# The scan of a hybrid backbone: where the next tile's raw products, its loads and the turned output stand

## The reference, cut to what matters

```python
def step(S, inp):
    r_t, w_t, k_t, v_t, kk_t, kka_t = inp
    sa = jnp.einsum('bdhvk,bdhk->bdhv', S, kk_t)
    S = (S * w_t[..., None, :] - sa[..., :, None] * kka_t[..., None, :]
         + v_t[..., :, None] * k_t[..., None, :])
    return S, jnp.einsum('bdhvk,bdhk->bdhv', S, r_t)
...
y = ys[:, :, 0] + jnp.flip(ys[:, :, 1], axis=1)
mu = jnp.mean(y, axis=-1, keepdims=True)
var = jnp.mean(jnp.square(y - mu), axis=-1, keepdims=True)
yn = ((y - mu) * lax.rsqrt(var + GN_EPS)).reshape(B, T, C) * lnx_w + lnx_b
```

## Time and profile before

| | us |
|---|---|
| median of 3 runs (4039.37 to 4051.58) | 4044.41 |
| the profiled execution, whole | 4038.96 |
| its span, first to last instruction | 4037.1 |
| scan stage, about | 955 to 1983 |
| merge stage, about | 1983 to 3240 |

### The profile page before, as it was taken

One profiled execution on the slowest core, in us unless ns is written; L12 is line 12 of the kernel. 1 busy time (PEld: TensorE's weight loads), 2 busy tenths in 40 slices (PEclk: granted clock), 3 DMA queues, 4 the chain that ended last, 5 costly groups with the idle time before them and its releaser, 6 DMA issues. The chain is left out here.

```text
span 4037.1 us, 64429 instructions
## 1 busy us (share of the span) xinstructions
PE 3634.8 (90%) x24967; PEld 2874.3 (71%) x24968; DVE 1380.7 (34%) x2811; ACT 748.8 (19%) x1399; POOL 1173.0 (29%) x1677
## 2 busy tenths in 40 slices
PE   8999999995688889889799999999999959999960
PEld 4666666663688888888788898998998944444430
DVE  2444444443344444444212222222122241222227
ACT  1222222222222322232101111111111001111113
POOL 0333333334566556655211101101101000000013
PEclk9999999997899999999899999999999969999985
DMA  8333323323332333232441101111111135665226
GB/s 286 105 104 104 104 99 104 104 85 107 95 94 60 97 100 92 62 97 74 144 171 40 63 35 40 63 35 45 58 40 54 50 119 197 241 232 192 94 101 216
DMA packets 297255, 424.33 MB, mean 105 GB/s; under 512 B 122446, under 2 KB 206156, under 8 KB 297036
## 3 DMA queue, kind: packets, MB, share of 16 engines
q1 hardware_dynamic: 278028, 351.79, 26.3%
q0 software_dynamic: 11952, 43.52, 3.3%
q10 hardware_dynamic: 7056, 25.69, 1.6%
HBM read 287.99 MB, written 132.94 MB: 104 GB/s over the span
## 5 line engine op out<-in xcount | busy, mean ns | idle before, releaser
L1761 PE MATMUL c_ps<-c_hT,big 128*128 128x128 f32 x6528 | 752.5, 276 | 25.3 <-DMA big<-in_w_in 25.3
L1761 PEld LDWEIGHTS c_ps<-c_hT,big 128*128 128x128 f32 x6528 | 743.8, 193 | 33.2 <-issue 29.5
L661 PE MATMUL a_ps<-a_win,a_hT 128*128 128x512 f32 (+1 forms) x1088 | 416.1, 540 | 3.5 <-DVE a_mix L572 3.5
L2184 PE MATMUL e_ps<-big,e_xT 128*128 x784 | 347.6, 597 | 2.3 <-DVE e_xT L2146 2.3
L661 PEld LDWEIGHTS a_ps<-a_win,a_hT 128*128 128x128 f32 x1088 | 204.1, 190 | 199.4 <-issue 187.0
L655 PE MATMUL a_ps<-a_hT,a_win 128*128 128x128 f32 x2992 | 343.5, 277 | 2.3 <-ACT a_hT L343 2.3
L655 PEld LDWEIGHTS a_ps<-a_hT,a_win 128*128 128x128 f32 x2992 | 340.2, 193 | 6.1 <-issue 2.9
L1095 POOL TENSOR_TENSOR b_tmp<-b_tt,b_ta 128x126 f32<-128x126 f32 (+22 forms) x527 | 203.1, 385 | 321.4 <-DMA b_ta<-s_a 266.7
L2184 PEld LDWEIGHTS e_ps<-big,e_xT 128*128 128x128 f32 x784 | 149.4, 191 | 191.7 <-issue 191.7
L1761 PE MATMUL c_ps<-c_wo,c_mT 128*128 128x512 f32 x544 | 236.3, 592 | 0.0
L1726 DVE TENSOR_TENSOR c_gs<-c_gs,c_ps 128x384 f32<-128x384 f32 x136 | 75.4, 554 | 444.8 <-PE c_ps L1761 434.5
(11 more groups left out here) (327 smaller groups left out, 5379.6 us busy)
## 6 DMA issues: line engine op xcount, KB each, us to landing
big<-in_exp_w SPq DMA_DIRECT2D x48, 1024.0 KB, 10.3
s_D<-a_shared SPq DMA_DIRECT2D x34, 768.0 KB, 5.8
b_f<-s_D SPq DMA_DIRECT2D x34, 768.0 KB, 7.2
s_yr<-e_yo ACTq DMA_DIRECT2D x49, 512.0 KB, 3.2
b_f<-s_A SPq DMA_DIRECT2D x34, 512.0 KB, 5.7
a_aw<-in_ada_w SPq DMA_DIRECT2D x32, 512.0 KB, 6.7
s_A<-a_shared SPq DMA_DIRECT2D x17, 768.0 KB, 3.4
big<-in_w_in SPq DMA_DIRECT2D x12, 1024.0 KB, 12.5
```

The source lines that it names most:

```text
L661: ins = nc.tensor.matmul(ps[:, bank, 0:width], hT[b][:, k, :], win[:, k, c:c + width], start=k == 0, stop=k == KD - 1)
L1761: return nc.tensor.matmul(out, lhsT, rhs, start=start, stop=stop)
L2184: return nc.tensor.matmul(out, lhsT, rhs, start=start, stop=stop)
```

## The change

It has four parts.

1. **The next tile's raw product stands at the head of a tile.** PE turns b and q of tile q+1, then r and k of tile q, forms `raw(q + 1)`, and then arb, aqk and ark of tile q. `b_ar` and `b_bT` have a second buffer each (`each2`); r goes through bank 0, k through bank 2, xx through bank 1. DVE transposes `b_ar` (AT) between the arb masks and the aqk masks. SP sends the diagonal blocks out right behind the inverse.
2. **`load_front` stands on ACT's queue**, in `front`, after `identity` and ahead of `b_xs`; it waits there for the same three things as on SP.
3. **The masked blocks**: AL5 is a plain copy of four 32-row blocks on ACT (`blocks`, after `b_u`), u6 reads `b_ar` itself, AL6 and POOL's `blocks` are gone.
4. **The output is made turned**: the moving operand of y is now the mix (`b_arkT`, `b_arbT`, 128 columns) and the weights are 64 columns of v or us; the two heads of a pair write to the two halves of PSUM's partitions. The stored tile is the transpose of before. In the merge, `turn_y` turns the sum of both directions back with four more transposes a tile; `scan_center` reads PSUM.

The diff, cut to its core:

```diff
-RT, BT, KT = each("rT", [P, 4, P]), each("bT", [P, 4, P]), each("kT", [P, 4, P])
-Ar, AT = each("ar", [P, H, P]), sb("b_at", [P, H, P])
-AL5, AL6 = each("al5", [P, H, P]), each("al6", [P, H, P])
+RT, KT, BT = each("rT", [P, 4, P]), each("kT", [P, 4, P]), each2("bT", [P, 4, P])
+Ar, AT = each2("ar", [P, H, P]), sb("b_at", [P, H, P])
+AL5 = each("al5", [P, H, P])
...
+def load_front(e, t, d):
+    e.dma_start(flat(F[d][:, 0:2, :]), tile_of(scr["A"], t)[:, 0:2 * W]).then_inc(f_in[d], 16)
+    e.dma_start(flat(F[d][:, 2:5, :]), tile_of(scr[f"D{d}"], t)).then_inc(f_in[d], 16)
...
             inverse_in(q)
+            if left > 0:
+                diagonal_out(q + 1, 1 - b)
...
-            if left > 1:
-                for d in range(2):
-                    sp.wait_ge(const_in, 48)
-                    after(sp, k_ok[d], q + 1)
-                    after(sp, b_ok[d], q + 1)
-                    after(sp, pm_ps[d], q + 1)
-                    load_front(two[d], d)
-            if left > 0:
-                diagonal_out(q + 1)
...
+        def front(t, tiles):
+            for d in range(2):
+                after(act, k_ok[d], t - 1)
+                after(act, b_ok[d], t - 1)
+                after(act, pm_ps[d], t - 1)
+                load_front(act, tiles[d], d)
...
+        def blocks(t, b):
+            for d in range(2):
+                for g in range(2):
+                    after(act, ar_ok[d][g], t)
+                    freed(act, u5_ps[d][g], t)
+                for c in range(2):
+                    first, second = slice(64 * c, 64 * c + 32), slice(64 * c + 32, 64 * c + 64)
+                    rows, cols = (second, first) if d == 0 else (first, second)
+                    a(AL5[d][rows, :, cols], Ar[d][b][rows, :, cols], ACT.Copy).then_inc(al5_ok[d], 1)
...
+            two = [tile_at(d, q + 2 if left > 2 else LAT) for d in range(2)]
+            if left > 2 and not isinstance(q, int):
+                two = [act.snap(t) for t in two]
             if left > 0:
                 turned(q + 1, 1 - b)
             for d in range(2):
+                after(act, kT_ps[d], q)
+                a(flat(KT[d][:, :, :]), bank(d, 2), ACT.Copy).then_inc(kT_ok[d], 1)
+            if left > 0:
+                raw(q + 1, 1 - b)
+                identity(q + 1)
+            if left > 1:
+                front(q + 2, two)
+            for d in range(2):
                 after(act, xx_ps[d], q)
-                a(Xs[d][:, :], bank(d, 0), ACT.Copy).then_inc(xs_ok[d], 1)
+                a(Xs[d][:, :], bank(d, 1), ACT.Copy).then_inc(xs_ok[d], 1)
+            for d, g in GROUPS:
+                after(act, u5_ps[d][g], q)
+                a(flat(U[d][:, heads(g), :]), bank(d, 2 * g), ACT.Copy).then_inc(u5_ok[d][g], 1)
             if left > 0:
-                raw(q + 1)
-                identity(q + 1)
+                blocks(q + 1, 1 - b)
...
+                if out is ArbT and left > 0:
+                    turn_raw(q + 1, 1 - b)
...
+            if isinstance(q, int) and q == 0:
+                for d, g in GROUPS:
+                    after(pe, ar_ok[d][g], 0)
+            if left > 0:
+                for d in range(2):
+                    turn_b(q + 1, 1 - b, d)
+                turn_q(q + 1, 0)
+            for d in range(2):
+                turn_r(d)
+            if left > 0:
+                turn_q(q + 1, 1)
+            for d in range(2):
+                turn_k(d)
+            if left > 0:
+                raw(q + 1, 1 - b)
+            for r in range(2):
+                for d in range(2):
+                    after(pe, (rT_ok, kT_ok)[r][d], q)
+                product(bT, RT, 2 * r, r, arb_ps)
+            for r in range(2):
+                for d in range(2):
+                    if left > 0:
+                        after(pe, ar_ok[d][in_round(d, r)], q + 1)
+                    else:
+                        freed(pe, (y_ok, pm_ok)[r][d], q + r)
+                product(KT, qT, 1 + 2 * r, r, aqk_ps)
...
-                    ins = mm(bank(d, 2)[lo, k * N:(k + 1) * N], AL6[d][hi, k, lo], TIT[d][hi, k, hi])
+                    ins = mm(bank(d, 2)[lo, k * N:(k + 1) * N], Ar[d][b][hi, k, lo], TIT[d][hi, k, hi])
...
-                    mm(bank(d, 1)[:, j * P:(j + 1) * P], RT[d][:, j, :], Shd[d][:, j, :], stop=False)
-                    for h in (2 * j, 2 * j + 1):
-                        own = slice(h * N, (h + 1) * N)
-                        mm(bank(d, 1)[:, own], ArkT[d][:, slot(h), :], V[d][b][:, own], start=False, stop=False)
-                        ins = mm(bank(d, 1)[:, own], ArbT[d][:, slot(h), :], Us[d][:, own], start=False, stop=h % 2 == 1)
+                    at = bank(d, 1)[:, j * P:(j + 1) * P]
+                    mm(at, Shd[d][:, j, :], RT[d][:, j, :], stop=False)
+                    for mix, val in ((ArkT, V[d][b]), (ArbT, Us[d])):
+                        for u in range(2):
+                            h = 2 * j + u
+                            ins = mm(at[64 * u:64 * u + 64], val[:, h * N:(h + 1) * N], mix[d][:, slot(h), :],
+                                     start=False, stop=mix is ArbT)
...
         def scan_center(t):
-            after(dve, s["ysum"], t)
-            v.reduce_sum(s8[0][:, :], by_head(ya[:, :]), axis=X_AXIS).then_inc(s["m_ok"], 1)
+            after(dve, s["yt_ps"], t)
...
+        def turn_y(t):
+            after(pe, s["ysum"], t)
+            freed(pe, s["yT_ok"], t)
+            for k in range(4):
+                ins = nc.tensor.transpose(ps[:, WB[1], k * P:(k + 1) * P], ya[:, k * P:(k + 1) * P], ident)
+            ins.then_inc(s["yt_ps"], 1)
...
+                if j == 2 and left > 0:
+                    turn_y(t + 1)
...
+                if i == 1 and left > 0:
+                    after(pe, s["yc_ok"], t + 1)
```

More of the change, by code:

```diff
@@ L880, in diagonal_out @@
                     after(sp, at_ok, t, 2)
-                    for d, tile in ((0, Ar[0]), (1, AT)):
+                    for d, tile in ((0, Ar[0][b]), (1, AT)):
                         for i in range(4):
@@ L929, in step @@
                     one = [tile_at(d, q + 1 if left > 1 else LAT) for d in range(2)]
-                    two = [tile_at(d, q + 2 if left > 2 else LAT) for d in range(2)]
                     past = [q - 1, 16 - q]
                     if left > 2 and not isinstance(q, int):
-                        one, two, past = ([sp.snap(t) for t in ts] for ts in (one, two, past))
+                        one, past = ([sp.snap(t) for t in ts] for ts in (one, past))
                     inverse_in(q)
+                    if left > 0:
+                        diagonal_out(q + 1, 1 - b)
                     for d in range(2):
@@ L993, in turned, with raw @@
                         a(flat(QT[d][b][:, :, :]), bank(d, 1), ACT.Copy).then_inc(qT_ok[d], 1)
-                    for d in range(2):
-                        after(act, bT_ps[d], t)
-                        a(flat(BT[d][:, :, :]), bank(d, 3), ACT.Copy).then_inc(bT_ok[d], 1)
-                def raw(t):
-                    freed(act, a_st, t, 128)
+                def raw(t, b):
+                    if not (isinstance(t, int) and t < 2):
+                        act.wait_ge(a_st, 128 * t - 128)
+                        for d in range(2):
+                            after(act, u6_ps[d], t - 2)
                     for r, pair in enumerate(PAIRS):
@@ L1019, in _ @@
                 turned(0, 0)
-                raw(0)
+                raw(0, 0)
+                act.wait_ge(clear_ok, 6)
+                blocks(0, 0)
+                front(1, [tile_at(d, 1) for d in range(2)])
                 for d in range(2):
@@ L1028, in step @@
                 def step(q, b, n, left):
-                    for d in range(2):
-                        after(act, kT_ps[d], q)
-                        a(flat(KT[d][:, :, :]), bank(d, 3), ACT.Copy).then_inc(kT_ok[d], 1)
+                    two = [tile_at(d, q + 2 if left > 2 else LAT) for d in range(2)]
+                    if left > 2 and not isinstance(q, int):
+                        two = [act.snap(t) for t in two]
                     if left > 0:
@@ L1042, in step @@
                             own_decay(q + 2, d)
-                    for d, g in GROUPS:
-                        after(act, u5_ps[d][g], q)
-                        a(flat(U[d][:, heads(g), :]), bank(d, 2 * g), ACT.Copy).then_inc(u5_ok[d][g], 1)
                     for d in range(2):
@@ L1070, in _ @@
                 for d in range(2):
-                    for tile in (Shd[d], TZ[d], AL5[d], AL6[d]):
+                    for tile in (Shd[d], TZ[d], AL5[d]):
                         g_.memset(tile[:, :, :], 0.0).then_inc(clear_ok, 1)
@@ L1364, in step @@
                             after(pe, aqk_ok[d][in_round(d, r)], q)
-                    if left > 0:
-                        turn_qb(q + 1, 1 - b)
-                    for d in range(2):
-                        after(pe, ark_ok[d][in_round(d, 0)], q)
                         after(pe, shd_ok[d], q)
```

148 lines of the change are left out of this document (51 added, 97 removed).

## The result

The changed kernel takes 4004.97 us in the median of 5 runs (4003.23 to 4019.33), the kernel before 4040.97 on the same chip: ratio 0.9913, 95% interval 0.9892 to 0.9935. That is 36 us faster, where 107 had been forecast (3938, range 3900 to 3998).

The account below looks back on a forecast made before the run. PE was taken to set the scan's pace. Savings of 9.4 (first tile) + 15 x (57.57 - 50.7) + 1.6 (last) - 7.5 (merge) = 106.6 us gave 3938 us, range for 8 in 10 3900 to 3998.

Parts of the forecast that it names:

- The gap ahead of w5: PE's large gap in a scan tile, ended by ACT's b_u: said to go, saving 4.53 us.
- the new wait ahead of xx: At the tile's head PE waits for DVE's aqk masks: 1.5 us, between 0 and 2.0.
- y: The turned output in each tile: 7.3 us instead of 8.93, with bounds of 5.4 and 10.8.
- PE's loop: PE's own work and waits over one scan tile: 50.7 us, from 59.18 in the tile shown.
- the slow clock: PE's low clock in w5 and u6 behind the gap: said to go with it, saving 1.5 us.
- The inverse's loop: One inversion's end to the next: 49.6 us, taken as 50.6 for the nearest tile; ends 47.2 and 57.9.
- wait 8 us for the inverse: In each tile u5 must wait until the inverse is back, 8 us after the inversion; nothing was taken for it.
- The first rival: The inverse's loop bounds the scan and is longer, its loads sharing DMA engines: 54.5 a tile, 3995 us, chance 0.22.
- the signs of being wrong: PE waiting at u5 in most tiles, diagonal blocks over 13 us, y over 9, or granted clock near 0.95.
- The first tile: PE waits for the first inverse in both kernels, then saves gap, slow clock and y: 9.4 us.
- The merge: Four more transposes a tile lose 17 x 0.44 = 7.5 us; their wait for POOL's sum costs nothing.
- The last tile: The scan's last tile, up to the merge: said to save 1.6 us.

Follow-up runs that it names:

- e5: Changed kernel with the loads of b_f (the front's loads) left out from the third tile on, but for one partition of 128: 3987.80 us, ratio 0.9858.
- e7: Changed kernel with the loads of b_f split: two rows at a tile's top, three while POOL inverts: 3995.36 us, ratio 0.9875.
- e1: Changed kernel with the eight products of queries with the state put ahead of the wait for the last aqk masks: 3993.85 us, ratio 0.9877.
- e2: Changed kernel with ACT issuing the loads of b_f once the solution has landed, and in the prologue ahead of the raw blocks: 3995.97 us, ratio 0.9881.
- e3: Changed kernel with the second tile's sum turned behind the sixth projection instead of the third, in the merge's first tile: 3989.19 us, ratio 0.9866.
- e9: e8 with the products with the state waiting for all four aqk masks again, still ahead of those with the values: 3938.12 us, ratio 0.9732.
- e11: Changed kernel plus e7's split loads and e3's edit, xx's products in turn, DVE turning the next raw blocks behind the aqk masks: 3915.58 us, ratio 0.9694.
- e8: Changed kernel with the split loads of e7 and the edits of e1 and e3 together: 3915.80 us, ratio 0.9685.
- e10: Changed kernel with e7's split loads and e1's edit, but y and merge of the kernel before: 3914.53 us, ratio 0.9686.

## Why the prediction was wrong

*The gap ahead of w5* went as said, and the new wait ahead of xx is 1.70 for 1.5 forecast. *y* takes 8.00 for 7.3 forecast, inside the bounds. The Trainium skill, TensorEngine Tiling (Array Packing), Tiling Modes, has a change of mode drain TensorE; the trace agrees, since two full passes take 0.42 until the narrow ones start, and the same two took 0.27 in y of the kernel before, where full-width ones follow. *PE's loop* by itself was nearly right: tiles without a slow clock (6, 8, 10 and 12) take 49.4, with a branch of 2.4 in every third 50.2, for 50.7 forecast.

Two steps failed, and each hides the other's cure.

1. "And, since PE then need not stop, the slow clock" was booked as a saving of 1.5 us. PE still stopped, 1.70 us ahead of xx, and there the clock fell instead. The step priced that wait at its own length (bounds 0 and 2.0) and not at what the products behind it cost at half clock: 4.9 us a time in xx and u5, in seven of the 15 tiles. By itself it holds the tile at 52.8 to 52.9 (e5, e7).
2. "The inverse's loop" of 49.6, taken as 50.6, has parts of 52.0 in the changed kernel: to the end of the solution's issue 9.3 for 8.2, from the first raw block to POOL's start 12.9 for 11.9, the inversion 29.8 for 29.5. And u5 was taken to wait 8 us for the inverse "anyhow", at no cost; the solution is back 16.4 us after the inversion, so that with a fast xx PE waits for it and the tile stays at 52.3 (e1). The rows of before had the loads of b_f behind b_tz in SP's queue; on ACT's queue they run beside it. Without the loads the parts sum to 47.6 (e5), near the lower end, 47.2. The Trainium skill, DMA: Bandwidth & Descriptors, Issuing engines are not separate DMA queues, says that both share the same DMA engines; the trace agrees (a median of 6.9 us to a landing of b_tz with the loads, 1.9 without).

The first rival named these shared engines and gave 3995, with a chance of 0.22, by a tile of 54.5. That its number lies near the measured time is in part luck: the tile was 53.0, the slow clock was not in it, and three smaller terms lost another 35 us that it had left as forecast. Of the signs of being wrong, the granted clock did stay at 0.95 in the scan; PE waits at u5 in only three tiles, since in seven others the slow xx gives the solution time.

Three smaller terms came out worse, the first tile and the last with the wrong sign. *The first tile*: "waits for the first inverse in both kernels" is true, but the first inverse comes 7.5 us later in the tile (1029.17 against 1019.05, in a tile that starts 2.6 later). The loads behind the raw blocks share the DMA engines with them and with the first solution; e2 and e7 take 8 and 9.5 us off this tile by the loads' place. *The merge*: "their wait for POOL's sum costs nothing" holds from the third tile on; for the second the load is issued only behind the merge's weights, and the wait is 14.29 us (e3 takes it away). 15 x 0.44 was right. *The last tile* ran part of its passes at half clock (xs's product 6.87 us to the next row, 3.62 before), and PE then waits 23.3 us for the merge's weights (21.8 before); which tile the half clock hits differs from kernel to kernel, and its cause was not tried.

Open: why tiles that start behind the loop's branch mostly keep their clock in xx (4, 6, 8, 10 and 12 of the changed kernel, but none in e2, not 6 and 8 in e3 and not 12 in e5). Where they lose it, the head behind the branch had run slow as well; tile 4 of the changed kernel had a slow head and kept the clock in xx.

## What to carry to other kernels

A new wait on TensorE can cost, besides its length, what the products behind it lose at the lower clock; price both, and see whether work without that dependence can go ahead of it or the wait be cut. When two loops are near each other in length, undo both suspects together as well as apart: here each alone was worth 0.2 to 0.7 us a tile and the pair 4.4. A transfer moved to another queue is no longer behind its neighbours but beside them; look for the short transfers of a dependent chain in that stretch.

## What the runs showed of the hardware that was not expected

The order of the same work can decide over the clock: 16 passes of 128 columns and 32 of 64 behind a wait of 1.70 us keep 2.4 GHz when the 128-column ones come first (e9, 15 of 15 tiles), and fall to 1.2 GHz when they alternate (e7, 9 of 15). Behind 0.51 us of wait the alternating order keeps it too (e11). Why the order matters was not tried. And a pause of 1.6 to 2.6 us for the loop's branch is followed by the slow clock in some tiles and not in others: in all five of e8 and e9, in one of five of e10 and of the changed kernel, in none of e7.

Small transfers on one queue are slowed by large ones on another: a 32 KB load of the solution lands in a median of 1.9 us without the front's loads and 6.9 beside them (e5 and the changed kernel).
